# Two parts of a preparation moved into the next program, and a bias table loaded by distance

## The reference, cut to what matters

```python
# the bonus and the gate of the recurrence (both directions d)
bonus = sum(rh * kd * r_k, axis=-1, keepdims=True) * vh
out_d = (head_norm(y_d) + bonus) * g_d          # out = out_0 + out_1
# the conformer convolution
h = u[..., :256] * sigmoid(u[..., 256:])
h = depthwise_conv(h, 31 taps) + dw_b
h = silu(layernorm(h, ln_g, ln_b))
# the neighbourhood attention: the bias depends on (key row - query row, key column - query column)
s_win = where(col_mask, q @ k + rpb[row distance, column distance], -inf)
```

## Time and profile before

| | |
|---|---|
| median of 3 runs | 2903.97 us |
| lowest, highest run | 2901.2, 2907.83 us |
| the profiled execution's own time | 2898.47 us |
| its span, first to last instruction | 2896.4 us |
| mean granted TensorE clock | 0.979 |
| layer 0: projection's program ends, attention starts | 769.8 us |
| layer 0: recurrence starts | 818.1 us |
| layer 1: projection's program ends, attention starts | 1677.6 us |
| layer 1: recurrence starts | 1716.5 us |

### The profile page before, as it was taken

The page is one execution under the profiler, slowest core; times in us unless marked ns, Lnnn a source line. Parts: engine busy times, 40 slices in busy tenths (PEclk is TensorE's granted clock), DMA queues, the critical chain, the costliest instruction groups (busy, mean ns, idle before and its releaser), DMA issues. The chain is left out here.

```text
span 2896.4 us, 55048 instructions
## 1 busy us (share of the span) xinstructions
PE 2732.7 (94%) x24339; PEld 1649.4 (57%) x24339; DVE 1015.3 (35%) x2097; ACT 437.9 (15%) x1000; POOL 178.5 (6%) x213
## 2 busy tenths in 40 slices
PE   8999999998888799999999878889999999999998
PEld 6668988744477464444684557745353453534435
DVE  3477475248654336650034755430000000000001
ACT  1311101113332110000023241110000000000001
POOL 0000000000134000000000024100000000000000
PEclk9999999999899899999999989989999999999999
DMA  7275575322300125533332230099999999999995
GB/s 252 99 247 169 184 243 183 126 87 87 60 3 3 59 88 198 194 129 101 109 126 86 87 61 3 12 344 375 334 401 336 376 372 341 396 337 379 366 345 203
DMA packets 187259, 572.06 MB, mean 198 GB/s; under 512 B 29168, under 2 KB 41836, under 8 KB 170650
## 3 DMA queue, kind: packets, MB, share of 16 engines
q1 hardware_dynamic: 164339, 506.94, 49.0%
q0 software_dynamic: 13856, 53.11, 5.1%
q10 hardware_dynamic: 8839, 8.59, 1.0%
HBM read 567.40 MB, written 1.23 MB: 196 GB/s over the span
## 5 line engine op out<-in xcount | busy, mean ns | idle before, releaser
L1127 PE MATMUL bank<-normed,weight_ring 128*128 128x256 f32 (+2 forms) x2528 | 669.1, 426 | 13.5 <-PEq L2226 8.2
L1127 PEld LDWEIGHTS bank<-normed,weight_ring 128*128 128x128 f32 x2528 | 456.7, 192 | 222.6 <-issue 180.4
L2776 PE MATMUL bank<-work 128*32 128x384 f32 (+1 forms) x3840 | 359.9, 529 | 0.0
L1127 PE MATMUL bank<-work,weight_ring 128*128 128x256 f32 (+2 forms) x1104 | 284.3, 417 | 4.2 <-PEq L1484 4.2
L687 PE MATMUL bank<-normed,weight_ring 128*128 128x512 f32 (+1 forms) x832 | 278.2, 494 | 0.0
L1127 PEld LDWEIGHTS bank<-work,weight_ring 128*128 128x128 f32 x1104 | 209.5, 192 | 74.8 <-issue 51.6
L2776 PEld LDWEIGHTS bank<-work 128*32 128x32 f32 x3840 | 122.3, 110 | 222.2 <-issue 222.2
L230 DVE SCALAR_TENSOR_TENSOR work<-work,small 128x512 f32<-128x512 f32 x336 | 237.6, 749 | 27.7 <-DMA work<-in_mod_w 20.6
L2776 PE MATMUL bank<-weight_ring,work 128*32 128x512 f32 (+1 forms) x2304 | 234.7, 561 | 10.0 <-issue 8.9
L687 PEld LDWEIGHTS bank<-normed,weight_ring 128*128 128x128 f32 x832 | 157.6, 190 | 118.5 <-issue 108.3
L2796 PE MATMUL bank<-work 128*32 128x256 f32 x3840 | 213.4, 379 | 0.0
(11 more groups left out here) (356 smaller groups left out, 2367.9 us busy)
## 6 DMA issues: line engine op xcount, KB each, us to landing
work<-in_moe_w_down SPq DMA_DIRECT2D x64, 1024.0 KB, 12.6
work<-in_mod_w POOLq DMA_DIRECT2D x48, 1024.0 KB, 5.9
work<-in_moe_w_gate SPq DMA_DIRECT2D x64, 768.0 KB, 4.9
weight_ring<-in_w_in SPq DMA_DIRECT2D x40, 1024.0 KB, 5.2
weight_ring<-in_moe_w_gate SPq DMA_DIRECT2D x32, 1024.0 KB, 15.0
work<-in_moe_w_gate SPq DMA_DIRECT2D x32, 1024.0 KB, 13.5
work<-in_moe_w_up SPq DMA_DIRECT2D x32, 1024.0 KB, 9.4
weight_ring<-in_moe_w_up SPq DMA_DIRECT2D x32, 1024.0 KB, 6.6
```

The costliest lines, as they stand in the source:

```text
L1127: last = nc.tensor.matmul(self.banks(gi)[j][:, to], w[:, k, j * P:(j + 1) * P], a, start=k0 + k == 0, stop=k0 + k == total - 1)
L2776: last = nc.tensor.matmul(self.bank[3 * up + a][g * R:(g + 1) * R, 0:n], xg[:, k, a * R:(a + 1) * R], w[:, g * n:(g + 1) * n], start=k == ...
```

## The change

Four things change.

- `Preparation` has 24 phases instead of 26. The bonus (phases 21, 22) and the norm (24, 25) leave its generators and become three generators, `late_tensor`, `late_vector` and `late_scalar`. `rwkv_scan` runs them as the `scan` of the first solve: one late step behind each two steps of the solve. They use the banks 4 to 7. The multiplication by the gates moves behind the norm. The buffers that they need (`a0`, `a1`, `ld1`, V) stay allocated over the attention; `tmp` now lies in `a0`.
- The bias is laid out by distance between rows. For each head and each of the two rows of queries in 128, 6 runs of 64 numbers are loaded instead of 4; the two query tiles read overlapping parts of it. There are 16 transfers instead of 32, and GpSimd adds the window (now 64 wide and broadcast over rows) in 4 instructions of 128x768 instead of 8 of 128x512.
- `load_weights` issues only two tiles ahead in the projection's program; the other two `w_out` tiles are issued in the attention's program, behind the bias.
- `pr`, `pt` and `bias` are taken from the arena as single buffers, so that they fit into the gaps.

```diff
+ROWS_APART = 6
@@ class Preparation
-        self.tmp = self.sh[:, 6:8, 0:self.nt]
+        self.tmp = self.a[0][:, :, 0:self.nt]
@@ def tensor: the bonus (p == BONUS) and the norm (p == NORM, NORM + 1) are removed
+    def late_tensor(self, pe):
+        nc, pr, B = self.nc, self.pr, self.pr.bank[4:8]
+        pe.wait_ge(self.bready.sem, self.bready.at(2))
+        for d in range(2):
+            for f in range(2):
+                last = nc.tensor.matmul(B[2 * d + f], pr.tab("headones"), self.a[d][:, f], start=True, stop=True)
+        last.then_inc(self.bsum.sem, 1)
+        yield
+        pe.wait_ge(self.tap.sem, self.tap.at(CV_LEN))
+        pe.wait_ge(self.chain.sem, self.chain.at(self.marks["bonus"]))
+        for f in range(2):
+            last = nc.tensor.matmul(B[0][:, 0:self.nt], pr.tab("ones"), self.o[:, f], start=f == 0, stop=f == 1)
+        last.then_inc(self.cvsum.sem, 1)
+        yield
+        pe.wait_ge(self.cvvar.sem, self.cvvar.at(1))
+        for f in range(2):
+            last = nc.tensor.matmul(B[1][:, 0:self.nt], pr.tab("ones"), self.tmp[:, f], start=f == 0, stop=f == 1)
+        last.then_inc(self.cvsum.sem, 1)
+        yield
+    def late_scalar(self, act):
+        yield
+        yield
+        act.wait_ge(self.cvinv.sem, self.cvinv.at(1))
+        nc.scalar.activation(self.tmp[:, 0], self.tmp[:, 0], ACT.Sqrt).then_inc(self.cvroot.sem, 1)
+        yield
+        act.wait_ge(self.cvdone.sem, self.cvdone.at(1))
+        for f in range(2):
+            last = nc.scalar.activation(self.o[:, f], self.o[:, f], ACT.Silu, bias=pr.col(f"ln_b{self.layer}", f))
+        yield
+    def late_vector(self, dve):
+        # step 1: wait bsum; ld[d][:, f] = B[2d+f] * v[:, f]                       (was L1012)
+        # step 2: wait cvsum 1; o = o - B[0] / 256; tmp = o * o                    (was L1024, L1027)
+        # step 3: wait cvsum 2; tmp = B[1] / 256 + eps; tmp = 1 / tmp              (was L1030, L1031)
+        # step 4: wait cvroot; o = o * gain * tmp                                  (was L1034)
+        # step 5: ld[d] = ld[d] * gate[d]; ld[0] = ld[0] + ld[1]                   (was L1017, L1019)
@@ def rwkv_scan
-                in_step(rec.solve_pe(pe, 0))
+                in_step(rec.solve_pe(pe, 0), prep.late_tensor(pe))
-                in_step(rec.solve_dve(dve, 0))
+                in_step(rec.solve_dve(dve, 0), prep.late_vector(dve))
-                in_step(rec.solve_act(act, 0))
+                in_step(rec.solve_act(act, 0), prep.late_scalar(act))
@@ def load_weights
-    def load_weights(self, sync):
-        while self.issued < min(len(self.weights), self.taken + WEIGHT_SLOTS):
+    def load_weights(self, sync, ahead=WEIGHT_SLOTS):
+        while self.issued < min(len(self.weights), self.taken + ahead):
@@ def head_attention
-                    for hd, (_, loads) in enumerate(bias_in["heads"]):
+                    for n_side, (_, loads) in enumerate(bias_in["sides"]):
                         for dst, src in loads:
-                            sync.dma_start(dst, src).then_inc(pair_in[hd // 2].sem, 16)
+                            sync.dma_start(dst, src).then_inc(pair_in[n_side].sem, 16)
+                    self.load_weights(sync)
-                    window = bias_in["shape"][0].unsqueeze(1).to_broadcast([P, 2, SEQ])
+                    window = bias_in["shape"][0].unsqueeze(1).to_broadcast([P, 2 * ROWS_APART, GRID_W])
-                        pool.wait_ge(q.sem, q.at(32 * len(loads)))
+                        pool.wait_ge(q.sem, q.at(16 * len(loads)))
@@ def block_two
-            prep = Preparation(self, layer, 26, prep_banks, seqs, lead)
+            prep = Preparation(self, layer, 24, prep_banks, seqs, lead)
-                    self.load_weights(sync)
+                    self.load_weights(sync, WEIGHT_SLOTS - 2)
-            bias = ar.take("bias", 8, 2, SEQ)
+            bias = [ar.take(f"bias{n}", 2, ROWS_APART * GRID_W) for n in range(4)]
+            for n in range(4):
+                seen = bias[n].rearrange("p h (r c) -> p h r c", r=ROWS_APART)
+                for h in range(2):
+                    for row in range(2):
+                        off = ((layer * 8 + 2 * n + h) * 15 + 5 - row) * 127
+                        loads.append((seen[row * GRID_W:(row + 1) * GRID_W, h],
+                                      bass.AP(self.rpb_dram, off, [[1, GRID_W], [127, ROWS_APART], [1, GRID_W]])))
```

More of the change, by code:

```diff
@@ L858, in tensor @@
-            if p == self.NORM:
-                pe.wait_ge(self.tap.sem, self.tap.at(CV_LEN))
-                pe.wait_ge(self.chain.sem, self.chain.at(self.marks["bonus"]))
-                for f in range(2):
-                    last = nc.tensor.matmul(B[0][:, 0:self.nt], pr.tab("ones"), self.o[:, f], start=f == 0, stop=f == 1)
-                last.then_inc(self.cvsum.sem, 1)
-            if p == self.NORM + 1:
-                pe.wait_ge(self.cvvar.sem, self.cvvar.at(1))
-                for f in range(2):
-                    last = nc.tensor.matmul(B[1][:, 0:self.nt], pr.tab("ones"), self.tmp[:, f], start=f == 0, stop=f == 1)
-                last.then_inc(self.cvsum.sem, 1)
@@ L907, in scalar @@
                 nc.scalar.activation(self.sq, self.sq, ACT.Sqrt).then_inc(self.rooted.sem, 1)
-            if p == self.NORM + 1:
-                act.wait_ge(self.cvinv.sem, self.cvinv.at(1))
-                nc.scalar.activation(self.tmp[:, 0], self.tmp[:, 0], ACT.Sqrt).then_inc(self.cvroot.sem, 1)
-                act.wait_ge(self.cvdone.sem, self.cvdone.at(1))
-                for f in range(2):
-                    nc.scalar.activation(self.o[:, f], self.o[:, f], ACT.Silu, bias=pr.col(f"ln_b{self.layer}", f))
             yield
```

144 lines of the change are left out of this document (75 added, 69 removed).

## The result

The kernel with the change takes 2866.11 us (median of four runs, 2864.95 to 2870.04) against 2902.65 for the kernel before on the same chip (four runs, 2901.2 to 2907.83): ratio 0.9875, 95% interval 0.9859 to 0.989. That is 36.5 us less. The forecast was -33.6 and 2870, its range 2857 to 2882. Run again beside other kernels, the changed kernel took 2866.13 (2864.04 to 2867.65), ratio 0.9883 (0.9866 to 0.9899).

The account below looks back on a forecast made before the run. TensorE, busy 94%, was taken as the bound, with gains only where it idles or a program outlasts its matmuls. Projection -46.6, solves +18.0, bias -5.0 gave -33.6: 2864.9 for the profiled execution, plus 5.5 for the median, 2870; range 2857 to 2882.

Parts of the forecast that it names:

- The walk through the first solve: Follows each engine's queue in program order through both layers' first solves; late work costs 11.5 and 6.5, together +18.0 us.
- a: First solve, TensorE: four bonus matmuls ahead of the W product delay the first level, +1.5 us, layer 1 +1.1.
- b: First solve, TensorE: two norm sums ahead of the level's second products, +1.7 us, layer 1 +0.9.
- c: First solve, VectorE: mean and square ahead of the level's additions, +1.5 us, layer 1 +0.4.
- d: First solve: TensorE's variance sums, then VectorE's scale and reciprocal ahead of additions; dearest place, +5.0 us, layer 1 +2.3.
- e: First solve: ScalarE's table loads, Sqrt and Silu and VectorE's gain hide in existing waits, 0 us.
- f: First solve, VectorE: gates and sum of the bonus, 3.61 us in a gap of 1.80, +1.8 us in each layer.
- rival E: Recurrence: TensorE idles about 3 us in the solve, falls to its lower clock and stays; 88 us, 2958, 4%.
- Rival B: First solve: square, gates and sum lock against GpSimd's picks over SBUF, 1.25 us each; +5 us, 2876, 13%.
- Rival D: First solve: more late work hides in its gaps, and the bias starts attention earlier; +9 instead of 18, 2861, 14%.
- C: First solve: the moved work is fully serial, +46.5 us instead of 18.0; 2899, no change to speak of, 4%.
- The bias: Attention: fewer, larger transfers and fewer GpSimd additions; layer 1 -3.5, layer 0 -1.5, together -5.0 us, bounds -9 and +2.

Follow-up runs that it names:

- spread kernel: Changed kernel with one late step behind every solve step instead of every two, and gain, gates, sum and Silu beside the second solve: 2858.05 us, ratio 0.9852.
- kernels of the first table: The kernel before, the changed kernel, and changed kernels with bonus and norm left out, only bonus late, only norm late, or only the bias changed: spans 2846.4 to 2898.1 us.
- experiment 4: Changed kernel with bonus and norm both put back into the projection's program, so only the bias and weight order change: 2898.59 us, ratio 0.9983.
- by head: Kernel with late work spread one step per solve step, plus eight GpSimd bias additions of 384, signalled per head, instead of four of 768: 2855.27 us, ratio 0.9846.
- by head, later: As by head, with the norm's square, its sums, scale, reciprocal halves and Sqrt one level later: 2852.65 us, ratio 0.9837.
- norm late: Changed kernel with the bonus put back into the projection's program, only the norm left beside the first solve: 2891.24 us, ratio 0.9963.

## Why the prediction came out

The projection's program came out as forecast, -24.7 and -21.9: by the profile's instructions, from the 26th tile's end to the attention's start, 53.26 became 28.52 and 50.41 became 28.52. The tiles ran back to back, the weights were there, VectorE was not late.

The walk through the first solve can be checked place by place, by how much later each level starts, counted from the first pair products:

| step | forecast L0 | measured L0 | forecast L1 | measured L1 |
|---|---|---|---|---|
| a, bonus sums ahead of level 1 | 1.5 | 1.58 | 1.1 | 1.95 |
| b, mean sums | 1.7 | 1.84 | 0.9 | 0.40 |
| c, mean and square on VectorE | 1.5 | 1.37 | 0.4 | -0.24 |
| d, variance sums, scale, reciprocal | 5.0 | 4.58 | 2.3 | 1.67 |
| e, Sqrt, gain, Silu | 0 | 1.08 | 0 | -0.23 |
| f, gates and sum of the bonus | 1.8 | 1.76 | 1.8 | 1.64 |
| last additions | 0 | 0.10 | 0 | -0.33 |
| sum | 11.5 | 12.31 | 6.5 | 4.86 |

Five of six places in layer 0 are right within some 0.4. The miss is e: not the table loads or the gain, which are still there in the kernel without the reciprocal and cost nothing in it, but TensorE at the lower clock behind the gap that d makes (0.66 granted over 5 us, the level's products 1.09 each instead of 0.66). The second profile has the same 1.05 there. That is rival E, in a piece of 5 us instead of the whole recurrence, whose granted clock was 0.94 against 0.95; it stays far from the 48 us at which it would decide. In layer 1 a to c together are right (2.1 against 2.4). There the kernel before ran at the lower clock into its first level; the 0.7 that I took off for it at a came off at b and c. Term d was 0.4 too high in layer 0 and 0.6 in layer 1. The sum is nearer than its parts: 0.8 too low in layer 0, 1.6 too high in layer 1. That these take each other off is luck.

Rival B, the lock in the solve: the moved instructions kept their times (1.22, 2.35, 1.29), so it cost them nothing here. But it is real: it appears as soon as an instruction with two SBUF operands falls beside a pick, as the square did in the spread kernel. It was the placement that spared the changed kernel: in layer 0 its square ran from 812.25 to 813.47, between picks that start at 809.06 and 815.59, and gates and sum ran behind the last pick, which ended at 825.12; only that pick began inside the gain, and took 1.37 instead of 1.27. The forecast had not worked this out, so it was luck too. Rival D had a mechanism that is right, the bonus in the solve's own wait, but the gates and the reciprocal did not hide. C is out with the table (its serial bound adds up to 46.3, not 46.5, which changes nothing).

The bias was mis-sized by these profiles: -6.7 instead of -5.0. How much of the 1.7 is real stays open, since layer 1's attention, with the same instructions, was 34.4 to 36.2 long in the kernels of the first table (36.22 where its first transfers landed 1 us later), and the bias alone gave 3.7 by whole times, or 5.0 without the 1.3 that the solve lost there. Layer 1 gave 4.4 instead of 3.5: the start came 2.15 earlier (9.57 to 7.42; forecast 1.5, the transfers came at the old pace in spite of their greater size), later waits for GpSimd went (1.2; forecast 0.9), and shorter multiplications gave (680 - 569) x 16 = 1.8 (forecast 1.1). These sum to 5.1, a little more than the length lost. Layer 0 gave 2.3 instead of 1.5, for which the forecast had no working, by the bias's layout and not by TensorE's clock (experiment 4). The multiplications became 0.8 shorter in all there; the other 1.5 I cannot put down to instructions one by one.

Of the 4.3 us between 2870.4 and 2866.1, the solves explain 0.8 (17.2 instead of 18.0) and the bias 1.7. The kernel before, timed again, was itself 1.3 lower than the median that I started from (2902.65 against 2903.97). The remaining 0.5 is within the spread of the runs.

## What to carry to other kernels

When work is moved beside a chain that goes from engine to engine, walk each queue in program order and pay only where the moved piece is longer than the engine's own idle time ahead of its next link: this gave 18.0 for 17.2 measured. Then cut and shift the pieces by the same table: a piece under the gap's length is nearly free, and the same work spread step by step cost 17.2 - 10.9 = 6.3 in the solves and 2.1 in the slices behind them. And read kernels of one family by stretches between common marks; whole spans carried up to 8 us of unchanged work, more than most of the effects here.

## What the runs showed of the hardware

VectorE and GpSimd hold each other up in SBUF: the one that comes second waits until the other's instruction is done. A TENSOR_SCALAR of 128x512 from SBUF to SBUF took 0.49 us alone, 1.28 when GpSimd's addition was under way, and ended 0.28 behind that addition's end. A product of two SBUF operands took 2.04 instead of 1.22 beside a pick. The work that was not moved shows it too, in both directions, in the solve of either kernel (timeline of the changed kernel):

```profile
803.06 1.26 POOL L510 TENSOR_TENSOR work<-work 128x512 f32<-128x512 f32 x1
803.23 1.63 DVE L457 TENSOR_TENSOR work<-work 128x512 f32<-128x512 f32 x1
804.28 1.71 POOL L511 TENSOR_TENSOR work<-work 128x512 f32<-128x512 f32 x1
```

VectorE's addition (L457) starts inside one pick and ends 0.54 behind it; the next pick starts inside that addition and takes 1.71 instead of 1.27. Instructions that read a bank and at most one SBUF operand kept 0.69. The forecast had this as a mean, 0.19 for each multiplication, and had put it under the rule for two SBUF operands; but these instructions have one. The Trainium skill (SBUF — State Buffer, "Who interferes with whom") calls it an exclusive lock and names `tensor_scalar` too among the operations that can take the shared ports. The trace agrees, with 353 and 487 ns on average without GpSimd's additions against 596 and 569 with them.

The same attention does not always take the same time. The kernels "by head" and "by head, later" have the same instructions there, and layer 0's was 43.92 in one and 46.06 in the other. The multiplications of 128x256 took 471 and 513 ns, which is 0.7 of the 2.1; TensorE's granted clock over the first 12 us was 0.86 in the one and 0.59 in the other, and it was busy 41.39 and 43.76 us. Which of the two decides is not shown. A change of a microsecond or two in such a stretch is no evidence from a single profile.

TensorE's clock fell to the lower level behind one gap of 2.79 us in an otherwise dense stretch, and came back within some 5 us, in both profiles of the changed kernel. A gap's length alone does not say it: behind the 2.94 ahead of the first level it stayed up in two kernels (before, and with bonus and norm left out) and fell in two (norm late, and bias alone), which cost those solves some 1.3. Behind the gap of 1.58, at 831.92, it fell once more in the first profile and not in the second, and behind that of 1.32 in neither. The second profile, behind 2.79 and behind 1.58 (length, busy time of the engines, clock, DMA share, GB/s), and then the first behind 1.58:

```profile
819.00:824.00 5.00, 4.59 (x110) 4.48 (x109) 2.77 (x5) 3.44 (x6) 1.27 (x1) 0.71 0.01 3
...
827.60:830.60 3.00, 2.43 (x64) 2.22 (x64) 1.31 (x3) 0.77 (x2) 0.00 (x0) 1.00 0.00 0
```

```profile
832.00:835.00 3.00, 2.79 (x64) 2.56 (x64) 0.96 (x3) 0.77 (x2) 0.00 (x0) 0.74 0.00 0
835.00:838.00 3.00, 2.59 (x64) 2.44 (x64) 1.02 (x3) 0.00 (x0) 0.00 (x0) 0.69 0.02 5
```
